# Compressing keys and values in three rounded products, with the weights standing

## The reference, cut to what matters

```
def _compress(tok, pos_emb, w):                 # tok: 1 x 256 x 2 x 128, w: 32 x 128 x 128
    chunks = tok.reshape(B, T // CMP_STRIDE, CMP_STRIDE, G, Dh)      # CMP_STRIDE = 16
    blocks = jnp.concatenate([chunks[:, :-1], chunks[:, 1:]], axis=2)  # 15 blocks of 32 tokens
    return jnp.einsum("bnlgd,lde->bnge", blocks + pos_emb[None, None, :, None, :], w)

k_cmp = _rms_norm(_compress(kc, cmp_pos_k, cmp_w_k), cmp_k_norm)
v_cmp = _compress(vc, cmp_pos_v, cmp_w_v)
```

## Time and profile before

| | us |
|---|---|
| median of three runs | 2262.01 (2261.34 to 2262.42) |
| the profiled execution's own time | 2261.14 |
| its span | 2259.4 |
| TensorE busy in the span | 2220.4 |
| VectorE busy | 1552.7 |
| ScalarE busy | 1086.9 |

### The profile page before, as it was taken

How to read it: one execution, slowest core, us unless ns; L and a number is a source line. 1 busy time by engine, 2 the same in 40 slices (tenths; PEclk the granted TensorE clock), 3 DMA queues, 4 the chain that set the end, 5 groups by cost and what they waited for, 6 DMA issues and landing times. The chain is left out here.

```text
span 2259.4 us, 29168 instructions
## 1 busy us (share of the span) xinstructions
PE 2220.4 (98%) x10164; PEld 1837.2 (81%) x10164; DVE 1552.7 (69%) x1990; ACT 1086.9 (48%) x1516; POOL 232.7 (10%) x216
## 2 busy tenths in 40 slices
PE   8999999999999999999999999989999999999998
PEld 7888877888888888888878887768888888888886
DVE  6455476877777778777866887977777444554456
ACT  5565463544444444344455776645444344434443
POOL 5003001000000000000001886000010000000000
PEclk9999999999999999999999999999999999999999
DMA  7656518798888888888856664867887666666664
GB/s 232 187 177 188 168 52 289 268 303 280 285 283 292 281 290 278 289 290 279 268 168 195 188 185 122 284 210 238 280 286 251 194 191 190 189 192 193 190 186 148
DMA packets 274500, 511.73 MB, mean 226 GB/s; under 512 B 20072, under 2 KB 28950, under 8 KB 274125
## 3 DMA queue, kind: packets, MB, share of 16 engines
q1 hardware_dynamic: 270252, 509.94, 71.3%
q10 hardware_dynamic: 4128, 0.26, 0.1%
HBM read 508.04 MB, written 2.10 MB: 226 GB/s over the span
## 5 line engine op out<-in xcount | busy, mean ns | idle before, releaser
L1909 DVE TENSOR_TENSOR w_lo<-raw,w_hi 128x1024 fp32r<-128x1024 f32 x760 | 944.1, 1246 | 539.8 <-ACT w_hi L1460 528.1
L1460 ACT ACTIVATE w_hi<-raw 128x1024 fp32r<-128x1024 f32 x760 | 802.4, 1060 | 952.1 <-PE bank L1025 892.4
L1041 PE MATMUL bank<-w_hi,act_hi 128*128 128x512 f32 x1984 | 776.0, 391 | 0.2 <-ACT w_hi L1460 0.2
L1042 PE MATMUL bank<-w_hi,act_lo 128*128 128x512 f32 x1984 | 772.3, 389 | 0.0
L1025 PE MATMUL bank<-w_lo,act_hi 128*128 128x512 f32 x2080 | 557.3, 390 | 0.0
L1025 PEld LDWEIGHTS bank<-w_lo,act_hi 128*128 128x128 f32 x2080 | 391.0, 188 | 82.6 <-DVE w_lo L1909 0.5
L1041 PEld LDWEIGHTS bank<-w_hi,act_hi 128*128 128x128 f32 x1984 | 372.5, 188 | 76.6 <-ACT w_hi L1460 0.6
L1042 PEld LDWEIGHTS bank<-w_hi,act_lo 128*128 128x128 f32 x1984 | 372.6, 188 | 76.0
L1041 PE MATMUL bank<-w_hi,mid_hi 128*128 128x512 f32 x960 | 376.0, 392 | 2.7 <-ACT w_hi L1460 2.0
L1042 PE MATMUL bank<-w_hi,mid_lo 128*128 128x512 f32 x960 | 373.7, 389 | 0.0
L1867 DVE SCALAR_TENSOR_TENSOR ada_acc<-ada_raw,c_act,ada_acc 128x512 f32<-128x512 f32 x360 | 269.8, 749 | 7.4 <-DMA ada_raw<-in_ada_w 0.4
(11 more groups left out here) (290 smaller groups left out, 1033.9 us busy)
## 6 DMA issues: line engine op xcount, KB each, us to landing
ada_raw<-in_ada_w SPq DMA_DIRECT2D x192, 512.0 KB, 5.1
raw<-in_w_gate SPq DMA_DIRECT2D x176, 512.0 KB, 4.5
raw<-in_w_up SPq DMA_DIRECT2D x176, 512.0 KB, 4.4
raw<-in_w_down SPq DMA_DIRECT2D x176, 512.0 KB, 4.5
...
```

The lines of the kernel that those rows point to most:

```text
L1041: pe.matmul(A_[t][:, :], h_, w_hi[:, s, kk, :], start=(k == 0), stop=False)
L1042: pe.matmul(A_[t][:, :], l_, w_hi[:, s, kk, :], start=False, stop=False)
L1460: act.activation(w_hi[:, U % SPLIT_SLOTS].rearrange("p k n -> p (k n)"), raw[:, R % RAW_SLOTS].rearrange("p k n -> p (k n)"), ACT.Copy).th ...
L1909: dve.tensor_tensor(w_lo[:, U % SPLIT_SLOTS].rearrange("p k n -> p (k n)"), raw[:, R % RAW_SLOTS].rearrange("p k n -> p (k n)"), w_hi[:, U ...
```

## The change

The tokens of `kc` and `vc` are no longer gathered by block. VectorE adds the position vectors of a block's first half (`ab = 0`) and of its second half (`ab = 1`) to all tokens, once each, in their own order (into `cost_mid` and `prob_mid`, which are free then); ScalarE rounds each into the high part, and VectorE forms the low part. So there are four additions, four subtractions and four ScalarE copies of 128 x 512 where there were eight additions of 128 x 240; they are spread over units 0 to 5 of chunk 9.

The weights of the compression now go through `split` as other weights do: eight more units (`CMP`), each 128 x 1024, each a ScalarE and a VectorE instruction. In `compress` the weights stand (128 x 128) and the tokens move, every 16th of a row. For each of 32 positions there are two instructions: the high weights by high and low tokens in one (2 x 2 groups x 16 = 64 columns), and the low weights by the high tokens (32 columns). That is 128 one-record products where there were 64 of two records. The result has the 128 entries on partitions and needs no turn for the keys: their squares are summed by a product with `ones` (32 columns, full float32), and the root is taken of a 128 x 32 tile. The values are repeated into `vrep` and turned by two transposes in iteration 6; `vcmp` is copied in iteration 7 instead of 5.

SyncE's loads of the weights behind the compression weights' slots now wait for `lo_done` (the split) instead of `cmp_used` (the products).

TensorE, iteration 3 of the attention, before: scores of job 3 (`fk,fq`), the turn of job 1, the values of job 0, then half of the value compression.

The diff, cut to its core:

```diff
     U_CMP = pos["U"]
+    pos["U"] += N_CMPU
+    CMP = [dict(R=R_CMP + 4 * kind, U=U_CMP + 4 * kind, C=None, nu=4, prev=None, ada=None, keep=None)
+           for kind in range(2)]
...
-        pick = sb("pick", [64, NSA_G, P], F32, begin)
-        blk_k = sb("blk_k", [P, CMP_BLOCK, 64], F32, begin)
-        blk_v = sb("blk_v", [P, CMP_BLOCK, 64], F32, begin)
+        vrep = sb("vrep", [P, NSA_G, P], F32, begin)
+        blocks = [sb(n, [P, 2, 2, NSA_G, T], F32R, begin) for n in ("blk_k", "blk_v")]
...
-                if R_CMP <= R < R_CMP + N_CMPU:
-                    sp.wait_ge(cmp_used, R - R_CMP + 1)
-                else:
-                    sp.wait_ge(lo_done, at((R if R < R_CMP else R - N_CMPU) + 1, r, stride))
+                sp.wait_ge(lo_done, at(R + 1, r, stride))
...
-                blk = (blk_k, blk_v)[kind]
-                pe.wait_ge(blk_zero, kind + 1)
-                pe.wait_ge(cum_copied, 1)
-                pe.wait_ge(blk_ready, 4 * (kind + 1))
                 for j in pieces:
-                    R = R_CMP + 4 * kind + j
-                    pe.wait_ge(raw_loaded[R % RAW_SLOTS], 16 * (R // RAW_SLOTS + 1))
-                    w = raw[:, R % RAW_SLOTS].rearrange("p a n -> p (a n)")
-                    for l in range(8):
-                        ins = pe.matmul(MISC[kind][0:64, 0:HD], blk[:, 8 * j + l, :], w[:, l * HD:(l + 1) * HD],
-                                        start=(j + l == 0), stop=(j == 3 and l == 7))
-                    ins.then_inc(cmp_used, 1)
+                    U = U_CMP + 4 * kind + j
+                    pe.wait_ge(hi_done, U + 1)
+                    pe.wait_ge(lo_done, U + 1)
+                    s = U % SPLIT_SLOTS
+                    for l_ in range(8):
+                        l = 8 * j + l_
+                        tok = blocks[kind][:, :, l // CMP_STRIDE, :, :].rearrange("p a g (n l) -> p a g n l",
+                                                                                  l=CMP_STRIDE)
+                        w_h = w_hi[:, s].rearrange("p a n -> p (a n)")[:, l_ * HD:(l_ + 1) * HD]
+                        w_l = w_lo[:, s].rearrange("p a n -> p (a n)")[:, l_ * HD:(l_ + 1) * HD]
+                        pe.matmul(MISC[kind][:, 0:64].rearrange("p (a g n) -> p a g n", a=2, g=NSA_G), w_h,
+                                  tok[:, :, :, :, l % CMP_STRIDE], start=(l == 0), stop=False)
+                        ins = pe.matmul(MISC[kind][:, 0:32].rearrange("p (g n) -> p g n", g=NSA_G), w_l,
+                                        tok[:, 0, :, :, l % CMP_STRIDE], start=False, stop=(l == CMP_BLOCK - 1))
+                    ins.then_inc(parts_used, 1)
 
...
+                    compress(0, (3,))
                     compress(1, (0, 1))
-                    pe.wait_ge(kc_n, 1)
-                    pe.transpose(MISC[0][:, T:T + 64], kcn[:, :], ident[0:64, 0:64]).then_inc(kc_turned, 1)
                 if i == 3:
+                    pe.wait_ge(kc_sq, 1)
+                    pe.matmul(MISC[0][:, 64:96], ones[:, :], kc_sum[:, 2, :], start=True, stop=True).then_inc(kc_summed, 1)
                     compress(1, (2, 3))
-                if i == 4:
-                    pe.wait_ge(vc_n, 1)
-                    pe.wait_ge(pick_made, NSA_G)
-                    for g in range(NSA_G):
-                        ins = pe.matmul(MISC[0][:, g * HD:(g + 1) * HD], pick[:, g, :], vcn[:, :], start=True,
-                                        stop=True)
-                    ins.then_inc(vc_spread, 1)
                 if i in (5, 6):
                     pe.wait_ge(kc_ready, 1)
+                    pe.wait_ge(vc_n, 1)
                     for h in range(4 * (i - 5), 4 * (i - 4)):
...
+                if i == 6:
+                    for g in range(NSA_G):
+                        ins = pe.transpose(MISC[0][:, g * HD:(g + 1) * HD], vrep[:, g, :], ident[:, :])
+                    ins.then_inc(vc_spread, 1)
                 if i == 10:
...
-            compress(0, range(4))
+            pe.wait_ge(cum_copied, 1)
+            pe.wait_ge(blk_lo, 4)
+            compress(0, range(3))
...
+                    if c is S_IN1[-2] and 1 <= u < 5:
+                        kind, ab = (u - 1) % 2, (u - 1) // 2
+                        act.wait_ge(blk_add, u)
+                        act.activation(blocks[kind][:, 0, ab, :, :].rearrange("p g t -> p (g t)"), full_of(kind),
+                                       ACT.Copy).then_inc(blk_hi, 1)
...
-                if i == 1:
+                if i == 0:
                     act.wait_ge(parts_used, LAST_U["in1"])
                     pre(LAST1, C_IN1, None)
-                    act.wait_ge(cmp_used, 4)
-                    link(act.activation(kcn[:, :], MISC[0][0:64, 0:HD], ACT.Square, accum_out=kc_ss[:, 0:1]))
-                    act.activation(kc_ss[:, 1:2], kc_ss[:, 0:1], ACT.Sqrt, bias=consts[0:64, 0:1],
+                    split(CMP[0], None, units=[3])
+                if i in (1, 2):
+                    split(CMP[1], None, units=[2 * i - 2, 2 * i - 1])
+                if i == 3:
+                    act.wait_ge(kc_summed, 1)
+                    act.activation(kc_rs[:, :], MISC[0][:, 64:96], ACT.Sqrt, bias=consts[:, 0:1],
                                    scale=1.0 / HD).then_inc(kc_std, 1)
...
+            split(CMP[0], None, units=range(3))
             attend(0, N_JOB1, probT1, row_min1, row_sum1, compressed)
...
-                kind, blk, src = ((0, blk_k, "kc"), (1, blk_v, "vc"))[u // 4]
-                g, j = u // 2 % 2, u % 2
                 n = TURNS.index(("plain", "kcvc", 0)) + 1
-                dve.wait_ge(turn_out_a, n)
-                dve.wait_ge(turn_out_d, n)
-                tok = heads[src][:, g, CMP_STRIDE * j:CMP_STRIDE * (j + N_CMP)].rearrange(
-                    "p (n l) -> p l n", l=CMP_STRIDE)
-                pc = pos_cols[:, kind * CMP_BLOCK + 16 * j:kind * CMP_BLOCK + 16 * j + 16]
-                dve.tensor_tensor(blk[:, 16 * j:16 * j + 16, 32 * g:32 * g + N_CMP], tok,
-                                  pc.unsqueeze(2).to_broadcast([P, 16, N_CMP]), ALU.add).then_inc(blk_ready, 1)
+                if u == 0:
+                    dve.wait_ge(turn_out_a, n)
+                    dve.wait_ge(turn_out_d, n)
+                if 2 <= u < 6:
+                    kind, ab = u % 2, u // 2 - 1
+                    dve.wait_ge(blk_hi, u - 1)
+                    dve.tensor_tensor(blocks[kind][:, 1, ab, :, :].rearrange("p g t -> p (g t)"), full_of(kind),
+                                      blocks[kind][:, 0, ab, :, :].bitcast(F32).rearrange("p g t -> p (g t)"),
+                                      ALU.subtract).then_inc(blk_lo, 1)
+                    dve.wait_ge(blk_lo, u - 1)
+                if u < 4:
+                    kind, ab = u % 2, u // 2
+                    n_b = T // CMP_STRIDE - ab
+                    pc = pos_cols[:, kind * CMP_BLOCK + CMP_STRIDE * ab:kind * CMP_BLOCK + CMP_STRIDE * (ab + 1)]
+                    src = heads[("kc", "vc")[kind]][:, :, CMP_STRIDE * ab:]
+                    dve.tensor_tensor(full_of(kind).rearrange("p (g t) -> p g t", g=NSA_G)[:, :, 0:T - CMP_STRIDE * ab].rearrange(
+                                          "p g (n l) -> p g n l", l=CMP_STRIDE),
+                                      src.rearrange("p g (n l) -> p g n l", l=CMP_STRIDE),
+                                      pc.unsqueeze(1).unsqueeze(1).to_broadcast([P, NSA_G, n_b, CMP_STRIDE]),
+                                      ALU.add).then_inc(blk_add, 1)
...
+                if i == 0:
+                    split(CMP[0], None, units=[3])
                 if i == 2:
+                    dve.wait_ge(parts_used, U_CMP + 4)
+                    link(dve.tensor_copy(kc_sum[:, 0, :], MISC[0][:, 0:32]))
+                    link(dve.tensor_tensor(kc_sum[:, 1, :], MISC[0][:, 32:64], kc_sum[:, 0, :], ALU.add))
+                    dve.tensor_tensor(kc_sum[:, 2, :], kc_sum[:, 1, :], kc_sum[:, 1, :], ALU.mult).then_inc(kc_sq, 1)
+                if i in (1, 2):
+                    split(CMP[1], None, units=[2 * i - 2, 2 * i - 1])
+                if i == 4:
                     dve.wait_ge(kc_std, 1)
-                    link(dve.reciprocal(kc_ss[:, 2:3], kc_ss[:, 1:2]))
-                    dve.tensor_scalar(kcn[:, :], MISC[0][0:64, 0:HD], kc_ss[:, 2:3], None, ALU.mult).then_inc(kc_n, 1)
-                if i == 3:
-                    dve.wait_ge(kc_turned, 1)
-                    dve.tensor_scalar(kcmpT[:, :], MISC[0][:, T:T + 64], cols[:, 83:84], None, ALU.mult).then_inc(
-                        kc_ready, 1)
-                    dve.wait_ge(cmp_used, 8)
-                    dve.tensor_copy(vcn[:, :], MISC[1][0:64, 0:HD]).then_inc(vc_n, 1)
-                if i == 5:
+                    link(dve.reciprocal(kc_rs[:, :], kc_rs[:, :]))
+                    dve.scalar_tensor_tensor(kcmpT[:, :].rearrange("p (g n) -> p g n", g=NSA_G)[:, :, 0:CMP_STRIDE],
```

(14 more changed lines are left out.)

26 lines of the change are left out of this document (11 added, 15 removed).

## The result

Time after: 2271.83 us, the median of 5 runs (2269.80 to 2275.27), against 2262.01 us before (5 runs, 2261.21 to 2262.63). Ratio 1.0044, 95% interval 1.0034 to 1.0055. The prediction said 2261.5 us in a range up to 2268.0: it was wrong by 10.3 us. The profiled execution of after is the run of 2275.27 us, the longest of the five, so its trace shows more than the median lost. The mean granted clock of the five runs is 0.990 or 0.991, where the profiled run of before has 0.996, so the clock was low in all five.

A forecast was written before the change was run, and what follows sets the result against it. TensorE was taken to bound the kernel: -15.25 + 13.70 + 0.21 + 0.20 + 0.30 + 0.33 = -0.51 us against the profiled 2261.14, 2260.6, then 2261.5 us for the runs' median; range 2259.3 to 2268.0.

The forecast's parts named there:

- the clock falls: Rival: thin compression pieces halve TensorE's clock; the last five pieces' 8.6 us double, 2270.1 us, or one episode, 2263.0; chance 0.09.
- 107 ns a record: TensorE's compression: each of 128 one-record products paced by its weight load, 13.70 us in all, 1.71 us a piece.
- The stride: Rival: strided token reads in TensorE's thin products outlast the load, a pair 333 ns instead of 214, +7.6 us; chance 0.11.
- The handoffs of the weights: Compression splits on ScalarE and VectorE ready before TensorE wants them, margins 0.3 to 2.7 us; later-handoffs rival: 2264 us, chance 0.10.
- The root: Key norms on ScalarE: table loads of 1.28 us each way, ScalarE occupied until 286.6, job 4's exponentials 0.2 us late.
- 0.30 us of wait ahead of the compressed scores: Attention iteration 5: TensorE waits for the repeated values from VectorE, ready at 289.35, wanted at 289.05; +0.30 us.
- the 0.33 of the `vcmp` copy: The copy moves from iteration 5 to iteration 7, right ahead of TensorE's wait at 301.17; counted whole, +0.33 us.
- the rest of the clock: Clock-fall cases slower by more than 4.5 us, the measurement's resolution; counted with the stride as 0.16.

The follow-up runs named there:

- cols1: The changed kernel with tokens written by position, so a position's columns lie side by side, each given once (64 and 32 moving columns): 2273.26 us, ratio 1.0047.
- cols4: As cols1, but each token column given four times (256 and 128 moving columns): 2262.80 us, ratio 1.0005 to the kernel before.
- contig: The changed kernel with thin products reading 32 neighbouring tokens instead of every 16th, so wrong tokens are multiplied: 2274.74 us, ratio 1.0054 to the kernel before.
- w4: The changed kernel with token columns given four times (256 and 128), stride of 16 kept: 2269.45 us, ratio 1.0035 to the kernel before.
- cols4e: cols4 plus one exponential of a constant on ScalarE right behind the root of the key norms: 2262.68 us, ratio 1.0001 to the kernel before.

## Why the prediction was wrong

- **The failed step** is the rival *the clock falls*, given 0.09, and with it the sum's unspoken term: that every one of the 128 records runs at the whole clock. The first three pieces did, the last five did not. The mechanism was named, with its place and nearly its shape ("behind the first three pieces ... for the other five"); cols1 and cols4, alike in all else, show that the number of moving columns decided it here. What spoke against it in the text was one stretch that streams as little, and it is 1.71 us long. In after the clock held through the first 5 us of thin pieces as well, so 1.71 us at 1.00 said nothing about 13.7. The other evidence, the fall behind 3.4 us of standing still, made a fall look like a matter of idle time. No row of before streams so little for so long, so the rows gave no ground for less than a tenth.
- **Its price** was 8.6 us. Against cols4 the five pieces took 17.06 in place of 9.26 us, 7.8 more, near enough. Missed was that the dense work between them runs at the lower clock too: 1.9, 3.6 and 3.3 us for the steps from 274.60, 286.76 and 297.21, where cols4 has 1.0, 1.8 and 1.7, and 0.5 until the clock was back, 4.9 in all. Together 12.7 us; less the wait of 1.07 us, which cols4 has and after hasn't, that is the 11.6 us between the two stretches (43.27 and 31.71).
- **The Trainium skill** ("TensorE: Matmul & The Clock Gate", section "HAM oscillation — how this bites in real kernels") warns of idle gaps as what re-throttles. In this trace there was none: busy 10.76 of 10.76 us at 0.50. Thin records last 0.28 us and start every 0.11 us in these rows, so a busy time of all the span says nothing of how many columns pass.
- **107 ns a record** was 112: 0.224 us a pair against 0.214, 64 x 0.010 = 0.6 us.
- **The stride** costs nothing in the thin form, as the sum had it (contig). The rival's mechanism is real though: 0.86 ns a column strided (w4), and it appears as soon as the load no longer covers it. What the prediction quotes of the Trainium skill ("SBUF — State Buffer", section "Door 1: The DMA port swizzle") agrees with TensorE's reads at a stride of 16 elements; no run has another stride.
- **The handoffs of the weights** were right: with the clock whole (cols4) no piece waits for a split.
- **The root** was mis-sized. It had the way back as part of one stretch ending at 286.6 and 0.2 us late, and 0.30 us of wait ahead of the compressed scores. In cols4 the load back starts at 287.98 and TensorE waits 1.07 us, which covers the 0.30; in cols4e the 1.07 is gone and the 0.30 is there. The Trainium skill ("ScalarE: Activation LUTs", section "Step-by-step: what each stage is for") puts a table load right before the ACTIVATE that needs it; the trace agrees, and one can't count on it ahead of time unless one asks for it.
- **The sum at whole clock.** Predicted for the stretch: -0.84 us (the -0.51 without the 0.33 of the `vcmp` copy, which comes later). cols4 has +0.57; cols4e, without the wait, -0.27. With 0.228 for 0.214 a pair (+0.90) the sum gives +0.06 for cols4e. The 0.33 that it is better than that lie mostly in the dense steps around the pieces, which take less from start to start than before (0.96 us for 1.18 in the first, 1.69 for 1.83 in the second) and which the sum took as unchanged. The time of cols4, 2262.80 beside 2262.78 for before, agrees with the total of -0.51, but its interval of 2 us either way can't tell it from none.
- **A slip in the chances.** Slower by more was the stride and the rest of the clock, 0.11 + 0.07 = 0.18, where the text has 0.16; with 0.82 and 0.02 the chances then add up to 1.02.
